# Attention on one Trainium2 core: the first scores of a step issued at the end of the step ahead

## The chip, the cores and the metric

The kernel runs on one core of a Trainium2 chip. The metric is the device time of one execution in microseconds (us); lower is better. Engines are named as in the profile: PE is TensorE (PEld its weight loads), DVE is VectorE, ACT is ScalarE, POOL is GpSimd, SP is SyncE.

## The reference

Two layers act on x of 1024 rows by 1024 columns. Cut to what matters here:

```python
for l in range(2):
    proj = rmsnorm(x, g_mix[l]) @ w_in[l]
    # A, 4 heads: softmax(q1 k1) - lam * softmax(q2 k2), all keys up to the row's chunk of 64
    # B, 4 heads: keys of a window of 128 and a sink logit
    # C, 4 heads: all keys up to the row, with a cumulated forget gate as bias
    x = x + concat([o_a, o_b, o_c]) @ w_out[l]
    h = rmsnorm(x, g_mlp[l])
    x = x + square(relu(h @ w_up[l])) @ w_down[l]
return rmsnorm(x, g_final)
```

Every softmax needs the maximum of its row of biased scores before the exponentials, and every product here is made of three fp32r products (high by high, high by low, low by high).

## The kernel before

Only the attention part of a layer is touched. It goes through 64 steps t. A step is one block of 128 query rows (i = t % 8) of one pair of score maps (t // 8): pairs 0 and 1 are group B, 2 and 3 group C, 4 to 7 group A. A row block i sees i + 1 key blocks of 128 (two at most in B), so a step has up to 1024 keys; above 512 keys its scores are made in two phases, since one map has one bank of PSUM per phase (`scores(t, 0)` and `scores(t, 1)`, line 1992).

For each step the work is: scores on PE (L2005, in C also a masked part, L2010); on DVE `biased_max` (line 1406: two L1428 instructions that add the bias, write the sum to `probs` and keep the row maximum, then L1443); on ACT two exponentials in place (L1040); on DVE in group A `combine` (L1451, L1453, L1456), which makes one map of the two; on PE transposes of the result (`turn_half`, L2058) by halves of at most four blocks; ACT copies a half as its high part (`half_high`, L1058), DVE makes the low part (`half_low`, L1479), PE multiplies by the values (`values`, L2078, L2088, L2090), and DVE sums the result (`sum_values`, L1494 in group A). In group C the result is folded on DVE first (`fold_values`, L1485) and turned on PE (`turn_values`, L2099) before it is summed.

The engines run in order, each by a list of slots that the program lays out ahead (the loop over `slots`). A slot is one half to be turned; a step has one to six slots, and the halves turned in the slots of step t are those of step t - 1. Group B and the short rows of A and C have one slot a step. `PIECES` spreads pieces of dense work over the slots: a piece is six 128x128 by 512 products (L1925) of the input projection for a later pair or of the output projection. In steps 53 to 55 and 61 of each layer (`MIX_AT`) further slots turn finished outputs for the output projection (L1053 on ACT, L1474 on DVE). After steps 51 and 58 (`SCALE_AT`) the variances of finished heads are made on DVE (L1510, L1513) and their root on ACT (L1080).

In a slot PE does: first scores if the slot is the step's first, one or two pieces, the second scores if it is theirs (`s.second`), the other pieces, `turn_values`, `turn_half` of this slot's half, `values` of the half turned one slot earlier. Pieces are split by

```python
early = max(min(2, len(s.pieces)), len(s.pieces) - 1)
```

DVE does in a slot: `biased_max(t, 0)` if first, `combine` or `invert_sums` of step t - 1 if first, the maxima of the second phase, low parts and evacuations of the projection, `half_low`, sums and folds, and in some steps the variances. ACT does, in steps with i of 4 and more, `half_high` ahead of the exponentials, in the others behind them and behind the sums' follow-up.

Semaphores that matter here: PE's scores of a phase wait until DVE has read the phase before it (`scores_read`; the two maps have one PSUM tile, ps[0]). `biased_max(t, ...)` waits until the last half of step t - 2 has been turned, since it overwrites that step's `probs`. `turn_half` in group A waits for `combined`, in B and C for the exponential; `turn_values` waits for `folded`; `values` waits for the low part.

Of the kernel before, what the change touches and what calls it, by code (L numbers as in the profile page):

```python
# [19 lines left out]
class Half:  # L20


    def __init__(self, index, step, units, slab=None, side=0):
        self.index, self.step, self.units, self.slab, self.side = index, step, units, slab, side
        self.blocks = sum(n for _, _, n in units)
        self.last = False
        self.used = None
        self.frees = 0


class Slot:


    def __init__(self, step, first, half):
        self.step, self.first, self.half = step, first, half
        self.values = None
        self.pieces, self.ends, self.ended, self.split = [], None, None, []
        self.turns_v = None
        self.summed = None
        self.unfold = None  # L40
        self.stored = None
        self.exps = []
        self.second = False


def hybrid_encoder(nc, x, w_in, a_lambda, a_subln, b_sinks, c_fbias, w_out, g_mix, g_mlp,
# [10 lines left out]
    NQ = S // P  # L57
# [55 lines left out]
    NT = PAIRS * NQ  # L113
# [86 lines left out]
    def folds(t):  # L200
        return ORDER[t // NQ][0] == "C"

    def load_of(done):
        return done if done < EXTRA else done + 1

    last = None
    for n, s in enumerate(slots):
        s.values = last.half if last and last.half and last.half.slab is None else None
        if s.values and s.values.last:
            s.summed = s.values.step  # L210
        s.unfold = last.summed if last and last.summed is not None and folds(last.summed) else None
        s.stored = []
        if last and last.unfold is not None:
            s.stored.append(last.unfold)
        if last and last.summed is not None and not folds(last.summed):
            s.stored.append(last.summed)
        if last and last.ends is not None:
            s.ended = last.ends
            n2 = load_of(last.ends + 2)
            slots[n + 2 if n2 == EXTRA + 1 else n].split.append(n2)  # L220
            if last.ends + 2 == EXTRA - 1:
                extra = slots[n + 3]
        last = s
# [46 lines left out]
    for g in range(STEPS):  # L270
# [7 lines left out]
        for name, spent in wanted:  # L278
            if kinds(g) == (P4, P4):
                t = 0 if name == "A22" else 3  # L280
            else:
                t, turn = turn % 4, turn + 1
# [15 lines left out]
    with ExitStack() as ctx:  # L298
# [980 lines left out]
        def _(dve):  # L1279
# [65 lines left out]
            for l in range(DEPTH):  # L1345
# [122 lines left out]
                def half_low(half):  # L1468
                    dve.wait_ge(pt_hi_done, NHALF * l + half.index + 1)
                    bank = bank_of(l, half)  # L1470
                    src = ps[2][:, BANK * bank:BANK * bank + half.blocks * P]
                    if half.slab is not None:
                        c = chunk_of(half.slab)
                        V.scalar_tensor_tensor(out=wide_lo[here][:, half.slab, at_slab(half)], in0=src,  # L1474
                                               scalar=mix_gain[:, NC * l + c:NC * l + c + 1],
                                               in1=wide_hi[here][:, half.slab, at_slab(half)].bitcast(F32),
                                               op0=ALU.mult, op1=ALU.subtract).then_inc(pt_split, 1)
                        return
                    V.tensor_tensor(pt_lo[:, bank, 0:half.blocks], src.rearrange("p (b q) -> p b q", q=P),  # L1479
                                    pt_hi[:, bank, 0:half.blocks].bitcast(F32), ALU.subtract).then_inc(pt_split, 1)  # L1480
# [45 lines left out]
                for s in slots:  # L1526
                    t = s.step
                    if s.first and t == 2 * NQ:
                        dve.wait_ge(cum_out, 16 * (l + 1))
                    if s.first and t < NT:  # L1530
                        biased_max(t, 0)
                    if s.first and t:
                        if ORDER[(t - 1) // NQ][0] == "A":
                            combine(t - 1)
                        else:
                            invert_sums(t - 1)
                    if s.turns_v is not None:
                        part_low(s.ended)
                    if s.second:
                        biased_max(t, 1)  # L1540
                    if s.ended is not None and s.ended < IN and s.turns_v is None:
                        part_low(s.ended)
                    if s.ends is not None:
                        if s.ends < IN:
                            evacuate(s.ends)
                        else:
                            add_out(s.ends - OUT)
                    if s.half:
                        half_low(s.half)
                    if s.unfold is not None:  # L1550
                        sum_values(s.unfold)
                    if s.summed is not None:
                        if folds(s.summed):
                            fold_values(s.summed)
                        else:
                            sum_values(s.summed)
                    if l == 0 and t == NQ and s.first:
                        lambdas()
                    if t in SCALE_AT and s.first:
                        variances(*SCALE_AT[t])  # L1560
                    if t - 1 in SCALE_AT and s.first:
                        invert_heads(*SCALE_AT[t - 1])
# [338 lines left out]
        def _(pe):  # L1901
# [40 lines left out]
            for l in range(DEPTH):  # L1942
# [71 lines left out]
                def dense(pieces):  # L2014
                    for s, c in pieces:
                        if s < IN:
                            if c == 0:
                                pe.wait_ge(w_split, LOADS * l + s + 1)
                                if SLABS[s - 1][1] == V_ and s > 4:
                                    pe.wait_ge(split_done, NSPLIT * l + s - 1)  # L2020
                                else:
                                    pe.wait_ge(evacuated, EVACS * l + s)
                            piece(s, c, 1)
                            continue
                        if c == 0:
                            pe.wait_ge(w_split, LOADS * l + s + 1)
                            if s == OUT:
                                pe.wait_ge(split_done, NSPLIT * l + NSPLIT)
                            else:
                                pe.wait_ge(evacuated, EVACS * l + s)  # L2030
                        if s == OUT:
                            pe.wait_ge(pt_split, NHALF * l + mix_ready[c])
                        j = w_slot(l, s)
                        mm = accumulate(1, w_hi[:, j, chunk_of(c)], w_lo[:, j, chunk_of(c)], wide_hi[here][:, c],
                                        wide_lo[here][:, c], c == 0, c == LATE - 1)
                        if c == LATE - 1:
                            mm.then_inc(slab_done, 1)
# [69 lines left out]
                for s in slots:  # L2107
                    t = s.step
                    early = max(min(2, len(s.pieces)), len(s.pieces) - 1)
                    if s.first and t < NT:  # L2110
                        scores(t, 0)
                    if s is slots[0]:
                        pe.wait_ge(evacuated, EVACS * l + 4)
                        turn(part, ps[3], NQ, v_turned)
                    if s.turns_v is not None:
                        pe.wait_ge(evacuated, EVACS * l + slab_of(s.turns_v, V_) + 1)
                        turn(part, ps[1], NQ, v_turned)
                    dense(s.pieces[:early])
                    if s.second:
                        scores(t, 1)  # L2120
                    dense(s.pieces[early:])
                    if s.unfold is not None:
                        turn_values(s.unfold)
                    if t == NT:
                        if s.first:
                            pe.wait_ge(scores_read, NPHASE * (l + 1))
                            pe.wait_ge(w_split, LOADS * l + EXTRA + 2)
                        for slab in (0, 1) if s.first else (2, 3):
                            out_piece(4, slab, 0, slab == 0, False)
                    if s.half:  # L2130
                        turn_half(s.half)
                    if s.values:
                        values(s.values)
# [161 lines left out]
```

## Time and profile before

| what | value |
|---|---|
| median of 3 runs | 2497.49 us (2489.79, 2498.4, 2497.49) |
| the profiled execution | 2490.63 us |
| its span, first to last instruction | 2488.5 us |
| PE busy, weight loads | 2379.5 us (96%), 1930.1 us (78%) |
| DVE busy | 1701.5 us (68%) |
| ACT busy | 1126.5 us (45%) |
| POOL busy | 260.3 us (10%) |
| mean granted clock of PE | 0.989 of full speed |
| the chain that ended last, by engine | PE 78%, DVE 9%, issue 4%, ACT 4%, DMA 2%, DVE's queue 2% |

Busy time is what an engine's instructions took, as a share of the span. The chain that ended last is followed back from the last instruction, at each step to what released it or to the instruction ahead of it on its engine. In the span, attention runs from about 69 to 556 us in layer 0 and from about 1300 to 1794 us in layer 1.

### The profile page before, as it was taken

Reading aid. Unit: us, or ns where it says so; the run is one execution under the profiler, and the core shown is the slowest. Engines: PE = TensorE matmul, PEld = TensorE weight load, DVE = VectorE, ACT = ScalarE, POOL = GpSimd, SP = SyncE. Lnnn points to the kernel's source line nnn. Section 1 sums busy time; section 2 is a strip of 40 time slices with the busy share of each in tenths; the row PEclk is TensorE's granted clock in tenths of the full one; section 3 lists DMA queues with packets and bytes.
Section 4 is the critical chain, followed back from the end, with each engine's and each line's share of the span. In section 5 each row is a group of like instructions: output and inputs, shape, how many; then the busy total and the mean of one; then the engine's idle time right before and its main releaser. Section 6 shows DMA issues by size and latency. Waiting matters only on the chain.

```text
span 2488.5 us, 32771 instructions
## 1 busy us (share of the span) xinstructions
PE 2379.5 (96%) x11857; PEld 1930.1 (78%) x11857; DVE 1701.5 (68%) x3128; ACT 1126.5 (45%) x2008; POOL 260.3 (10%) x286
## 2 busy tenths in 40 slices
PE   8999999899899999999999999998999999999998
PEld 6877777678788887888888777776787888788886
DVE  5555666666877779888636556666577777797872
ACT  5554444554544444333436545454454444433334
POOL 1111011123000000000321111121220000000002
PEclk9999999999999999999999999998999999999999
DMA  5211001211354458868331100102115544687753
GB/s 183 68 27 26 18 26 34 69 52 35 115 199 157 143 198 260 259 199 257 127 94 26 26 26 21 31 26 68 56 44 168 186 145 156 235 266 237 221 177 102
DMA packets 291400, 296.58 MB, mean 119 GB/s; under 512 B 19702, under 2 KB 236832, under 8 KB 290984
## 3 DMA queue, kind: packets, MB, share of 16 engines
q1 hardware_dynamic: 285440, 278.74, 35.3%
q10 hardware_dynamic: 5800, 15.75, 1.7%
q8 instruction: 95, 1.56, 0.3%
q14 instruction: 65, 0.53, 0.1%
HBM read 214.20 MB, written 80.25 MB: 118 GB/s over the span
## 4 chain that ended last, share of the span: by engine, by line
PE 78%; DVE 9%; issue 4%; ACT 4%; DMA 2%; DVEq 2%; SPq 1%; ACTq 0%; POOL 0%; POOLq 0%
PE ps L1925 25%; PE ps L2192 18%; PE ps L2244 8%; PE ps L2246 8%; PE ps L2245 8%; PE ps L2058 3%; PE ps L2005 3%; PE ps L2088 2%; PE ps L2078 1%; DVE probs L1428 1%; ACT pt_both L1058 1%; DVE probs L1456 1%; ACT probs L1040 1%; PE ps L2090 1%; DMA a_raw<-in_w_up_dram 1%
## 5 line engine op out<-in xcount | busy, mean ns | idle before, releaser
L2244 PE MATMUL ps<-b_hi,d_hi 128*128 128x512 f32 x896 | 351.1, 392 | 10.9 <-DVE b_lo L1721 6.5
L1925 PE MATMUL ps<-wide_hi,w_hi 128*128 128x512 f32 x1024 | 337.4, 411 | 13.5 <-DVE c_parts L1367 5.5
L2245 PE MATMUL ps<-b_lo,d_hi 128*128 128x512 f32 x896 | 350.1, 391 | 0.0
L2246 PE MATMUL ps<-b_hi,d_lo 128*128 128x512 f32 x896 | 349.7, 390 | 0.0
L1925 PE MATMUL ps<-wide_lo,w_hi 128*128 128x512 f32 x1024 | 320.1, 394 | 0.0
L1925 PE MATMUL ps<-wide_hi,w_lo 128*128 128x512 f32 x1024 | 318.5, 392 | 0.0
L1479 DVE TENSOR_TENSOR pt_both<-ps,pt_both 128x512 fp32r<-128x512 f32 (+3 forms) x216 | 126.5, 586 | 222.8 <-ACT pt_both L1058 222.1
L1162 ACT ACTIVATE d_hi<-d_raw 128x1024 fp32r<-128x1024 f32 x112 | 118.3, 1058 | 340.9 <-DVE d_raw L1705 110.4
L1058 ACT ACTIVATE pt_both<-ps 128x512 fp32r<-128x512 f32 (+3 forms) x216 | 110.4, 511 | 337.9 <-PE ps L2058 337.5
L1040 ACT ACTIVATE probs<-probs,neg_max,slope 128x256 f32<-128x256 f32 (+7 forms) x256 | 202.3, 791 | 95.2 <-DVE neg_max L1443 74.9
L883 POOL TENSOR_TENSOR w_lo<-w_raw,w_hi 128x256 fp32r<-128x256 f32 x216 | 158.2, 764 | 830.1 <-ACT w_hi L933 830.1
L1925 PEld LDWEIGHTS ps<-wide_lo,w_hi 128*128 128x128 f32 x1024 | 193.9, 189 | 43.8
L1925 PEld LDWEIGHTS ps<-wide_hi,w_lo 128*128 128x128 f32 x1024 | 193.3, 189 | 43.3
L1925 PEld LDWEIGHTS ps<-wide_hi,w_hi 128*128 128x128 f32 x1024 | 175.7, 190 | 64.7 <-issue 34.0
L2244 PEld LDWEIGHTS ps<-b_hi,d_hi 128*128 128x128 f32 x896 | 168.7, 188 | 50.4 <-DVE d_lo L1716 7.2
L2192 PE MATMUL ps<-t_hi,a_hi 128*128 128x512 f32 x472 | 188.6, 400 | 11.5 <-ACT c_rows L1140 6.6
L2246 PEld LDWEIGHTS ps<-b_hi,d_lo 128*128 128x128 f32 x896 | 169.0, 189 | 35.6
L2245 PEld LDWEIGHTS ps<-b_lo,d_hi 128*128 128x128 f32 x896 | 168.9, 189 | 34.7
L2192 PE MATMUL ps<-t_hi,a_lo 128*128 128x512 f32 x472 | 185.6, 393 | 0.0
L2192 PE MATMUL ps<-t_lo,a_hi 128*128 128x512 f32 x472 | 185.1, 392 | 0.0
L1716 DVE TENSOR_TENSOR d_lo<-d_raw,d_hi 128x1024 fp32r<-128x1024 f32 x112 | 139.8, 1249 | 41.2 <-ACT d_hi L1162 41.1
L1129 ACT ACTIVATE c_rows<-c_rows 128x512 f32<-128x512 f32 x120 | 75.7, 631 | 177.7 <-DVE c_rows L1657 176.3
(212 smaller groups left out, 4476.4 us busy)
## 6 DMA issues: line engine op xcount, KB each, us to landing
d_raw<-in_w_down_dram SPq DMA_DIRECT2D x112, 512.0 KB, 6.3
b_raw<-b_saved SPq DMA_DIRECT2D x112, 512.0 KB, 6.6
a_raw<-in_w_up_dram SPq DMA_DIRECT2D x60, 512.0 KB, 4.1
b_saved<-c_rows SPq DMA_DIRECT2D x118, 256.0 KB, 3.0
w_raw<-in_w_in_dram SPq DMA_DIRECT2D x92, 256.0 KB, 3.3
b_saved<-far SPq DMA_DIRECT2D x30, 512.0 KB, 4.3
w_raw<-in_w_out_dram SPq DMA_DIRECT2D x36, 256.0 KB, 3.0
x_saved<-xt ACTq DMA_DIRECT2D x16, 512.0 KB, 3.4
```

Of the source, the lines that this page charges most:

```text
L883: low = nc.gpsimd.tensor_tensor(w_lo[:, j, c:c + 2], w_raw[:, c:c + 2], w_hi[:, j, c:c + 2].bitcast(F32), ALU.subtract)
L1040: e = A.activation(probs[:, (2 * t + j) % 4, 0:width], probs[:, (2 * t + j) % 4, 0:width], ACT.Exp, bias=neg_max[:, at:at + 1], scale=sl, ...
L1058: A.activation(pt_hi[:, bank, 0:half.blocks], src.rearrange("p (b q) -> p b q", q=P), ACT.Copy).then_inc(pt_hi_done, 1)
L1129: A.activation(c_block[l][b], c_block[l][b], ACT.Square).then_inc(u_squared, 1)
L1162: A.activation(d_hi[u % 3][:], d_raw[t][:], ACT.Copy).then_inc(d_hi_done, 1)
L1479: V.tensor_tensor(pt_lo[:, bank, 0:half.blocks], src.rearrange("p (b q) -> p b q", q=P), pt_hi[:, bank, 0:half.blocks].bitcast(F32), ALU.s ...
L1716: V.tensor_tensor(d_lo[u % 3][:], d_raw[t][:], d_hi[u % 3][:].bitcast(F32), ALU.subtract).then_inc(d_split, 1)
L1925: mm = T.matmul(ps[p][:, bass.ts(t, BANK)], w, h[:, bass.ts(t, BANK)], start=(start and n == 0), stop=(stop and n == 2))
L2192: mm = T.matmul(out, w, h[:, c], start=(start and c == 0 and k == 0), stop=(c == NC // 2 - 1 and k == 2), skip_group_check=not start)
L2244: T.matmul(out, w0, b0, start=first, stop=False)
L2245: T.matmul(out, w0, b1, start=False, stop=False)
L2246: mm = T.matmul(out, w1, b0, start=False, stop=last)
```

## The change

For every step t with t % 8 other than 0 and t < 64 (56 steps in each layer) the first scores of the step are issued in the last slot of step t - 1: on PE behind that slot's pieces, ahead of its `turn_values`, `turn_half` and `values`. Their maxima are taken in the same slot on DVE: behind its `half_low` and ahead of its sums and folds. The first slot of step t leaves both out. Nothing else is moved; no instruction is added or left out.

```diff
+        self.early = None
+        self.scored = False
...
+        if s.first and s.step < NT and s.step % NQ:
+            last.early, s.scored = s.step, True
...
-                    if s.first and t < NT:
+                    if s.first and t < NT and not s.scored:
                         biased_max(t, 0)
...
                     if s.half:
                         half_low(s.half)
+                    if s.early is not None:
+                        biased_max(s.early, 0)
                     if s.unfold is not None:
                         sum_values(s.unfold)
...
-                    if s.first and t < NT:
+                    if s.first and t < NT and not s.scored:
                         scores(t, 0)
...
                     dense(s.pieces[early:])
+                    if s.early is not None:
+                        scores(s.early, 0)
                     if s.unfold is not None:
                         turn_values(s.unfold)
```

## Rows read from the trace of the kernel before

**Rows 1.** PE's waits: engine, line, whom it waited for, us in total, times, longest.

```profile
PE ps L2058 <- DVE probs L1456: 19.9, 24, 1.9
PE ps L2099 <- DVE fold L1485: 11.2, 12, 2.7
...
PE ps L2005 <- DVE row_max L1428: 6.2, 8, 1.5
```

**Rows 2.** DVE's waits, the line of the maxima.

```profile
DVE probs L1428 <- issue: 44.0, 61, 4.8
```

**Rows 3.** Timeline, a half of four blocks, steps 36 and 37: start, us, engine, line.

```profile
326.55 0.60 PE L2058 MATMUL ps<-ident_r,probs 128*128 128x128 f32 x4
...
327.19 0.60 ACT L1058 ACTIVATE pt_both<-ps 128x512 fp32r<-128x512 f32 x1 [4.76 <-PE ps L2058]
...
327.81 0.69 DVE L1479 TENSOR_TENSOR pt_both<-ps,pt_both 128x512 fp32r<-128x512 f32 x1 [0.56 <-ACT pt_both L1058]
...
330.57 0.89 DVE L1456 SCALAR_TENSOR_TENSOR probs<-probs,lam_ratio 128x640 f32<-128x640 f32 x1
...
332.11 0.66 PE L2058 MATMUL ps<-ident_r,probs 128*128 128x128 f32 x4
```

**Rows 4.** Timeline, a half of one block, steps 37 and 38.

```profile
334.91 0.27 PE L2058 MATMUL ps<-ident_r,probs 128*128 128x128 f32 x1
...
335.52 0.29 DVE L1479 TENSOR_TENSOR pt_both<-ps,pt_both 128x128 fp32r<-128x128 f32 x1 [1.07 <-ACT pt_both L1058]
...
335.98 0.50 PE L2005 MATMUL ps<-k_hi,q_hi 64*128 64x512 f32 x2
...
336.88 0.73 PE L1925 MATMUL ps<-wide_hi,w_hi 128*128 128x512 f32 x2
...
337.00 0.69 DVE L1428 CUSTOM_DVE_ANT_0 probs<-ps,far 128x512 f32<-128x512 f32 x1 [1.18 <-issue]
...
339.97 0.63 PE L2058 MATMUL ps<-ident_r,probs 128*128 128x128 f32 x4 [0.74 <-DVE probs L1456]
```

**Rows 5.** Timeline of PE, four waits in last slots (steps 20, 28, 29, 61).

```profile
181.01 0.44 PE L2099 MATMUL ps<-ident_r,fold 128*128 128x128 f32 x2 [0.28 <-DVE fold L1485]
...
259.03 0.44 PE L2099 MATMUL ps<-ident_r,fold 128*128 128x128 f32 x2 [1.43 <-DVE fold L1485]
...
270.13 0.74 PE L2078 MATMUL ps<-pt_both,c_parts 128*128 128x256 f32 x4 [1.18 <-DVE pt_both L1479]
...
530.25 0.39 PE L2088 MATMUL ps<-v_parts,pt_both 128*128 128x256 f32 x1 [1.04 <-DVE pt_both L1479]
```

**Rows 6.** Timeline, folds and the turns that wait for them, steps 18 to 27.

```profile
167.85 0.68 DVE L1485 TENSOR_REDUCE fold<-ps 128x256 f32<-128x512 f32 x1
...
170.74 0.38 PE L2099 MATMUL ps<-ident_r,fold 128*128 128x128 f32 x2
...
243.07 0.68 DVE L1485 TENSOR_REDUCE fold<-ps 128x256 f32<-128x512 f32 x1
...
244.24 0.38 PE L2099 MATMUL ps<-ident_r,fold 128*128 128x128 f32 x2
...
249.48 0.44 PE L2099 MATMUL ps<-ident_r,fold 128*128 128x128 f32 x2 [2.69 <-DVE fold L1485]
```

**Rows 7.** Timeline of ACT and DVE, steps 59 and 60.

```profile
511.04 1.28 ACT L1040 ACT_TABLE_LOAD   x1
...
514.36 0.47 ACT L1058 ACTIVATE pt_both<-ps 128x384 fp32r<-128x384 f32 x1
...
515.78 0.69 DVE L1428 CUSTOM_DVE_ANT_0 probs<-ps,far 128x512 f32<-128x512 f32 x1
...
518.98 0.35 DVE L1428 CUSTOM_DVE_ANT_0 probs<-ps,far,row_max 128x128 f32<-128x128 f32 x1 [0.16 <-issue]
```

**Rows 8.** Windows: stretch, us, busy (x) of PE, PEld, DVE, ACT, POOL, PEclk, DMA, GB/s.

```profile
451.50:455.00 3.50, 3.49 (x17) 3.50 (x18) 2.03 (x7) 2.26 (x7) 3.50 (x6) 0.51 0.00 0
478.60:482.00 3.40, 2.01 (x14) 1.32 (x14) 3.15 (x10) 0.70 (x2) 0.22 (x1) 1.00 0.59 166
```

## The prediction

> **What bounds the kernel now.** I read the page first: PE is busy 2379.5 us of the 2488.5 us span, so all idle time of PE is 109 us, and nothing that leaves PE's own work alone can win more. The table of PE's waits then says what part of it this change can reach [rows 1]: 19.9 us in 24 waits of the transposes for `combine`, 11.2 us in 12 waits for folds, 6.2 us in 8 waits of second scores for the maxima of the first phase. That is 37.3 us over both layers, 1.5% of the time. DVE's table shows 44.0 us of idle time in front of the maxima, 61 times [rows 2]: DVE was free and PE had not yet made the scores. That is what moving the scores forward speaks to. Whether it helps has to be read from the timeline, slot by slot, because DVE works in order and its list hardly changes: the maxima stood directly behind `half_low` and the last slot's sums already, and are now only put ahead of those sums. On PE the scores change places with `turn_half` and `values` of one slot. So the question is which of two chains feeds the maxima last.
>
> **The change part by part.** The instructions stay the same, no DMA is moved, and SP's and POOL's queues are not passed; all that is to be priced is waiting.
>
> The basic exchange. First scores of 512 keys take 0.97 us (335.98 to 336.95; six matmuls) and a piece 1.4 us (336.88 to 338.3) [rows 4]. Before, the maxima began when `turn_half`, `values` and scores had all gone through PE; now they begin when scores, `turn_half`, `half_high` and `half_low` are through. For a last half of four blocks [rows 3]: the turn ends at 327.15, ACT takes 0.60, DVE 0.69, so `half_low` ends at 328.50. With scores first, all three come 0.97 later, so the maxima start at about 329.45 where they started at 328.76, and the exponentials of step 36, which ACT has behind `half_high`, are late too. `combine` ended at 331.46 with its turn at 332.11, a margin of 0.65; the sum in front of it does not get shorter, so it ends about 1.1 later, near 332.55, and PE waits about 0.5 to 0.6: a wait where none was. For a last half of one block [rows 4]: `half_low` ended at 335.81, the maxima waited 1.18 us until 337.00. Scores first, the short half is ready by about 336.5, half a us earlier, and the 0.74 us wait at 339.97 and the one of the second scores ahead of it shrink by about as much. Following the four-slot pattern through steps 37, 38 and 39 (and 45 to 47 alike) I get +0.6, -0.5, +0.1 us: **+0.2 us** for each of two pairs.
>
> Waits that the moved scores fill. In a last slot PE now has 0.97 us more to do ahead of `turn_values` and `values`. Four waits a layer lie there [rows 5]: 0.28 us at 181.01 is filled whole, of the 1.43 at 259.03 about 0.95, of the 1.18 at 270.13 about 0.85 (the turn comes late by that much, but ACT reaches it no sooner). Of the 1.04 at 530.25 some 0.9 is filled, but `combine` of step 61 does not move and is waited for next, so 0.5 is kept. **-2.6 us.**
>
> Folds behind the maxima. Where a step of group C has one slot, the fold stands behind the early maxima: 1.3 us, L1443 with its drain 0.5, and 0.97 for the turn that is late. The fold at 167.85 ends at 168.53, its turn starts at 170.74, a margin of 2.2; the fold now ends near 171.65. PE waits 0.95 and then the chain of step 20's second scores carries it on: **+0.9 us.** The fold at 243.07 has a margin of 0.5 only [rows 6]; it ends near 246.85, a wait of 2.4 us at 244.24. But 2.69 us were lost at the next turn, at 249.48, because `half_high` stood behind two exponentials; these start only 0.5 later, so most of that wait has gone by. I get the turn at 250.35 with step 28's first scores done, where it was 249.48 with them to come: **-0.95 us** for the two.
>
> Root, table load and the second maxima, steps 59 and 60. This is the largest term. In step 58's slot the variances now stand behind the maxima of step 59 (1.3 us, L1443 0.3) and behind a `half_low` that is 0.4 late: 2 us. ACT's root waits for them, its load of the exponential's table (1.28 us, from 511.04) follows, and then two exponentials and `half_high` at 514.36 [rows 7], all 2 us later. So `half_low` and the maxima of step 60 go from 515.78 to about 517.4. And step 60 has its second scores and the early scores of step 61 in one slot with two pieces, both of which stand ahead of the second scores: step 61's scores wait for the second maxima of step 60, which stand behind `combine` of step 59 on DVE (518.98 before [rows 7], about 521.1 now). PE waits until about 521.8 with `turn_half`, `values`, dense pieces and through them `half_low` queued behind. The turn starts near 522.65; it was 518.96, and the scores, which then came behind it, are 0.97: 2.7 us lost here. One slot on, `half_low`, maxima and `combine` in a row are late by 1 us more. **+3.7 us.** In steps 36, 44 and 52 one piece lies between the two scores; its 1.4 us covers the second maxima, with 0.4 us to spare in the first.
>
> Steps 51 to 54. In step 51 the variances are behind the maxima too, second maxima of step 52 end 0.3 late for PE, and `half_high` and with it the exponentials of step 52 come 1.3 later; the 1.9 us wait, the longest on `combine` [rows 1], grows by as much: **+1.3 us.** In step 54 a mix half of four blocks is the last: **+0.4 us.** In step 55 ACT is last as before: 0. Groups B and the steps with three pieces have more than 2 us of cover for the late half: 0; without it each of these would cost up to 0.5.
>
> The clock. Behind the 1.9 us wait [rows 1] the granted clock is 0.51 from 451.5 to 455.0, the lower level of 1.2 GHz; behind the longest wait on the maxima, 1.5 us [rows 1] up to 478.6, it stays at 1.00 [rows 8]. The half-speed stretch costs about 1.7 us of 3.5. The wait of some 2.4 us before step 61's scores has no row of its own; it is nearer to the first of the two, but it need not hit, so I take half: **+0.9 us**; bounds 0 and 1.7, and with the longer waits of steps 27 and 53 up to 3.4. The Trainium skill ("TensorE: Matmul & The Clock Gate", the part on HAM oscillation) speaks of longer gaps than any named here as what costs the clock. By it this term is 0 and the sum 1.8 us lower. The trace does not agree, by its row behind the 1.9 us wait.
>
> **Sum** for a layer: 0.4 - 2.6 + 0.9 - 0.95 + 3.7 + 1.3 + 0.4 + 0.9 = +4.05 us; layer 1 shows the same waits (12 of the 24, 6 of the 12), so **+8.1 us**, 0.33%. Against the profiled execution this is 2490.6 + 8.1 = 2498.7. That execution was 6.9 us under the median of the runs shown, and the four times lie in two groups, 2490 and 2498; their mean is 2494.1. I put the sum on that mean: **2502 us**.
>
> **The rivals.** (a) The exchange is a gain where I read a loss: DVE's 44 us of idle time goes, and with it most of the 37.3 us of [rows 1]. If only the terms that gain count and half of the `combine` and maxima waits (13 us) go too: 2.6 and 0.95 twice is 7.1, in all -20 us, 2474. For it: 61 idles. Against it: the half of one block is the only kind in which `half_low` was long done. (b) Slower by a new wait at one place: early scores behind the second maxima, in single-slot steps 36, 44, 52 and 60. It decides once `combine` ends later than one piece behind the second scores. Step 60 has no piece; if the three others also lose 1 to 1.5 us each, and the clock drops behind each, this adds 3 to 5 us a layer: 2510 to 2513 on the mean. (c) The change does nothing, since DVE's order is almost what it was, and step 60's table load is hidden after all: 2494, within 2 us.
>
> **How the numbers follow.** My forecast, a small loss of 4 to 12 us, has 0.5; (c) with what lies around it, down to -10 us, 0.24; (a) 0.1; (b) 0.16. A difference of 0.5% (12.5 us) is about what a measurement of this kernel can tell from no change. Faster than that takes (a): 0.1. Slower takes (b) in full: 0.16. Within: 0.74. The range goes from 2486 (a gain of 4 on the lower group) to 2513 (b's end).
>
> **What would show it.** Right, if PE's waits for folds include one of over 2 us near step 27, if PE's L2005 waits for `far_max` of L1428 in step 60 (there is no such wait now), if the variances of step 58 (L1510, L1513) start only behind the L1443 of step 59, and the table load with them, and if DVE's idle time ahead of L1428 falls far below 44 us while the waits for L1456 do not fall by more than a third. Wrong, if the waits for L1456 fall below 8 us, or if step 60's turn is not late by 2 us or more against step 57's.

## The result and the profile after

The changed kernel takes 2508.26 us in the median of 6 runs (2505.92 to 2511.84); the kernel before took 2494.73 us in 6 runs on the same occasion. The ratio is 1.0065, 95% interval 1.0051 to 1.0078: slower by 12.7 to 19.5 us (the two medians alone lie 13.5 us apart). The forecast, 2502 in a range of 2486 to 2513, had the sign and held the time; its sum of +8.1 us was about half of what came.

The page of the changed kernel, its span and busy times:

```profile
span 2504.0 us, 32771 instructions
## 1 busy us (share of the span) xinstructions
PE 2386.3 (95%) x11857; PEld 1925.1 (77%) x11857; DVE 1700.6 (68%) x3128; ACT 1127.6 (45%) x2008; POOL 261.1 (10%) x286
```

The instructions are the same in number, and the span is 15.5 us longer. It parts in two. PE idle is 2504.0 - 2386.3 = 117.7 us where it was 2488.5 - 2379.5 = 109.0: **8.7 us more waiting**. PE busy is up by **6.8 us** with the same matmuls: these took longer. The forecast had 6.3 us of waits and 1.8 us of clock.

The stretch of attention in both layers, before and then changed, between the same instructions (columns as in [rows 8]):

```profile
69.30:556.10 486.80, 455.89 (x2679) 363.05 (x2680) 305.73 (x919) 250.86 (x589) 79.91 (x109) 0.99 0.13 39
1300.00:1794.00 494.00, 464.77 (x2711) 371.04 (x2710) 303.22 (x904) 248.12 (x582) 77.08 (x105) 0.99 0.13 36
```

```profile
69.30:561.80 492.50, 459.08 (x2679) 360.33 (x2680) 305.27 (x919) 251.35 (x589) 80.30 (x109) 0.98 0.13 38
1306.00:1809.00 503.00, 469.17 (x2712) 369.24 (x2711) 303.08 (x904) 248.69 (x582) 77.49 (x105) 0.98 0.12 36
```

The layers lost 5.7 and 9.0 us there. Waits are 2.5 and 4.6 of it, 7.1 in all; the other 1.6 of the 8.7 us lie outside what was changed. PE's busy time makes 3.2 and 4.4, 7.6 in all, at a lower granted clock.

PE's waits of the changed kernel, to be read against [rows 1] (lines are shifted by 4 to 8: L1460 is `combine`, L1432 the maxima, L1489 the fold, L1044 an exponential, L2064 the transposes, L2011 scores, L2105 the turn of a fold, L2094 values):

```profile
PE ps L2064 <- DVE probs L1460: 22.4, 30, 2.5
PE ps L2011 <- DVE row_max L1432: 14.0, 19, 1.5
...
PE ps L2094 <- DVE pt_both L1483: 4.6, 8, 1.0
PE ps L2105 <- ACT probs L1044: 4.6, 2, 2.3
...
PE ps L2105 <- DVE fold L1489: 4.1, 10, 0.8
...
PE ps L2011 <- DVE far_max L1432: 3.4, 2, 1.7
```

The waits for folds fell from 11.2 us to 4.1, with 4.6 beside them that are put down to an exponential: 2.5 us won. The waits of values fell. But the waits for `combine` did not fall (22.4 where 19.9 were), those for the first maxima more than doubled (14.0 for 6.2), and the wait for the second maxima, `far_max`, is new. DVE's own table shows what the change did do:

```profile
DVE probs L1432 <- issue: 18.5, 26, 3.3
```

DVE's idle time ahead of the maxima is down from 44.0 us to 18.5 [rows 2]. None of the 25.5 us came out as time. They were DVE's and not PE's.

Timeline of the changed kernel in steps 36 and 37, the steps of [rows 3]:

```profile
323.12 0.50 PE L2011 MATMUL ps<-k_hi,q_hi 64*128 64x512 f32 x2
...
324.02 0.66 PE L2064 MATMUL ps<-ident_r,probs 128*128 128x128 f32 x4
...
325.35 0.69 DVE L1483 TENSOR_TENSOR pt_both<-ps,pt_both 128x512 fp32r<-128x512 f32 x1 [1.61 <-ACT pt_both L1062]
325.96 0.69 DVE L1432 CUSTOM_DVE_ANT_0 probs<-ps,far 128x512 f32<-128x512 f32 x1
...
328.10 0.89 DVE L1460 SCALAR_TENSOR_TENSOR probs<-probs,lam_ratio 128x640 f32<-128x640 f32 x1
...
329.13 0.63 PE L2064 MATMUL ps<-ident_r,probs 128*128 128x128 f32 x4 [0.46 <-DVE probs L1460]
```

Read it from turn to `combine`: 324.02 to 328.10 is 4.08 us; before, it was 326.55 to 330.57, 4.02 us [rows 3]. The chain turn, `half_high`, `half_low`, maxima, sum, `combine` is as long as ever. It starts 0.9 us later against PE's own list, since the scores now stand in front of the turn, and a wait of 0.46 us stands where a margin of 0.65 was.

### The profile page after: what moved, and what is told of

Its sections match the earlier page's. It is cut to its first block, busy times and chain, and to the rows that moved or that the text cites. A ratio compares the mean times of both kernels' runs of the same rounds, so it can differ in the third digit from the quotient of the medians.

```text
span 2504.0 us, 32771 instructions
## 1 busy us (share of the span) xinstructions
PE 2386.3 (95%) x11857; PEld 1925.1 (77%) x11857; DVE 1700.6 (68%) x3128; ACT 1127.6 (45%) x2008; POOL 261.1 (10%) x286
## 4 chain that ended last, share of the span: by engine, by line
PE 77%; DVE 10%; issue 4%; ACT 4%; DMA 2%; DVEq 2%; SPq 1%; ACTq 0%; POOL 0%; POOLq 0%
PE ps L1931 23%; PE ps L2200 18%; PE ps L2252 8%; PE ps L2253 8%; PE ps L2254 8%; PE ps L2064 4%; PE ps L2011 3%; PE ps L2094 2%; DVE probs L1432 1%; ACT pt_both L1062 1%; DVE probs L1460 1%; DMA d_raw<-in_w_down_dram 1%; PE ps L2084 1%; PE ps L2096 1%; ACT probs L1044 1%
## 5 line engine op out<-in xcount | busy, mean ns | idle before, releaser
L2252 PE MATMUL ps<-b_hi,d_hi 128*128 128x512 f32 x896 | 351.2, 392 | 10.4 <-DVE b_lo L1727 6.3
L1044 ACT ACTIVATE probs<-probs,neg_max,slope 128x256 f32<-128x256 f32 (+7 forms) x256 | 202.2, 791 | 73.0 <-DVE neg_max L1447 57.3
```

The source lines that it names most:

```text
L1044: e = A.activation(probs[:, (2 * t + j) % 4, 0:width], probs[:, (2 * t + j) % 4, 0:width], ACT.Exp, bias=neg_max[:, at:at + 1], scale=sl, ...
L2252: T.matmul(out, w0, b0, start=first, stop=False)
```

## The experiments

In the diffs, the two lines that issue the early scores on PE, and the two that take their maxima on DVE, are those of the change. All ratios are to the kernel before, measured beside the run. "Idle" is PE's, span less busy of the profiled execution; before it is 109.0 us.

**One group of steps at a time.** The first of two, group C alone:

```diff
-        if s.first and s.step < NT and s.step % NQ:
+        if s.first and s.step < NT and s.step % NQ and ORDER[s.step // NQ][0] == "C":
```

> Early scores only for the steps of group C (i 1 to 7 in pairs 2 and 3, 14 steps a layer); A and B as before. My theory (the loss is made in group A by scores ahead of the turn, and by the clock): PE's waits fall by 1 to 2 us a layer against the kernel before, with fold waits at 8 to 9 us where they were 11.2 and the waits of values (L2078, L2088) down by 2 us a layer; the time is 2 to 5 us below before, 0.998 to 0.9995, if the half-speed stretches do not grow. Rival (maxima ahead of the folds are what costs): fold waits above 11 us and the time 3 us or more above before. Rival (the early scores cost wherever they stand, as PE changes its pattern): half of the 15.5 us, 7 us above before.

Measured: 0.998 (0.9965 to 0.9995), median 2488.99 us; idle 106.9. Group C alone is a gain, as forecast. Its fold waits (4.1 us, and 4.6 put down to the exponential) are those of the changed kernel; of the waits of values, group C's own 2.4 us (L2084, before L2078) are gone, 1.2 a layer and not 2: those on L2094, 7.7 us, are group A's. The second, group A alone (the same line with "A"):

> Early scores only for the steps of group A (28 a layer); B and C as before. My theory: the whole loss is here and more than whole, since C gained: 16 to 20 us above before, ratio 1.0065 to 1.008, with the wait for far_max (L1428) of 1.7 us a layer, a combine wait of 2.5 us near step 53 and at least 10 us more time at half speed than before. Rival (the fold order costs): no more than 8 us above before.

Measured: 1.0047 (1.0031 to 1.0064), 2505.95 us; idle 119.4, 10.4 above before. The loss is in group A, with the `far_max` wait (3.4 us in 2) and the longest `combine` wait (2.5 us) as said, but 11.7 us is less than the 16 to 20 I named. With C's -5 and A's +11.7 us the parts add to +6.7, under the whole's +16; the intervals are some 4 us wide each side and group B, which was not run alone, adds something (below). The waits do add up: idle -2.1 and +10.4, the whole +8.7. What is missing shows in the granted clock, as the mean over all executions of a kernel: 0.989 before and in group C alone, 0.987 in group A alone, 0.985 in the changed kernel.

**Where the scores stand on PE.**

```diff
-                    if s.early is not None:
-                        scores(s.early, 0)
                     if s.unfold is not None:
                         turn_values(s.unfold)
...
                     if s.half:
                         turn_half(s.half)
+                    if s.early is not None:
+                        scores(s.early, 0)
                     if s.values:
                         values(s.values)
```

> The early scores are issued behind turn_half of the last slot, ahead of its values, instead of ahead of both; DVE's list as in the changed kernel. My theory: what makes the maxima late is that the turn of the last half, and with it half_high, half_low and in the later steps the exponentials, stand 0.97 us behind the scores. With the turn first, combine waits fall from 22.4 us to 10 to 14 us and row_max waits from 14.0 to under 7; steps 59 to 61 keep about 2.5 us a layer of their loss (table load behind the variances). The time is 10 to 16 us under the changed kernel: 2492 to 2498, ratio to before 0.999 to 1.002. Rival (the loss is DVE's order, or the fixed pattern of PE): within 4 us of the changed kernel, 1.005 and more.

Measured: 0.9967 (0.9949 to 0.9984), 2485.52 us, faster than before and some 23 us under the changed kernel. Idle 98.2. Its waits:

```profile
PE ps L2064 <- DVE probs L1460: 19.9, 24, 2.0
...
PE ps L2094 <- DVE pt_both L1483: 6.2, 8, 1.1
PE ps L2105 <- DVE fold L1489: 5.9, 12, 1.5
```

The waits for the first maxima are 4.6 us in 4, none for `far_max`. The theory held, and more strongly than I had put it: the ratio lies below the range I gave. One number missed the other way: waits for `combine` are 19.9 and not 10 to 14. Timeline of the same steps as above:

```profile
321.78 0.60 PE L2064 MATMUL ps<-ident_r,probs 128*128 128x128 f32 x4
...
323.04 0.69 DVE L1483 TENSOR_TENSOR pt_both<-ps,pt_both 128x512 fp32r<-128x512 f32 x1 [0.56 <-ACT pt_both L1062]
...
325.80 0.88 DVE L1460 SCALAR_TENSOR_TENSOR probs<-probs,lam_ratio 128x640 f32<-128x640 f32 x1
...
327.42 0.66 PE L2064 MATMUL ps<-ident_r,probs 128*128 128x128 f32 x4
```

Turn to `combine` is 4.02 us again, and the next turn comes with a margin, as before the change. The same kernel once more, since it beats both:

> The third run's kernel once more, in more rounds, since it may beat both kernels. My theory: ratio to before 0.9955 to 0.998, 5 to 11 us under before. Rival (its first result was the clock's luck in the executions drawn): 0.999 to 1.001.

Measured: 0.9964 (0.9951 to 0.9978), 2483.29 us; idle 98.9. The first result was not luck.

**DVE's order.** PE as in the changed kernel, the early maxima behind sums, folds and variances:

```diff
                     if s.half:
                         half_low(s.half)
-                    if s.early is not None:
-                        biased_max(s.early, 0)
...
                     if t - 1 in SCALE_AT and s.first:
                         invert_heads(*SCALE_AT[t - 1])
+                    if s.early is not None:
+                        biased_max(s.early, 0)
```

> PE as in the changed kernel; on DVE the early maxima stand behind the slot's sums, folds and variances instead of ahead of them, so DVE's list is that of the kernel before. My theory: this takes back the table load's lateness in steps 59 to 61 (2 to 2.5 us a layer) and the new fold waits, but gives the maxima 0.4 us later in group A: 4 to 8 us under the changed kernel, ratio to before 1.003 to 1.005; the wait for far_max stays, at 0.7 to 1.2 us. Rival (DVE's order is the whole loss): back to before, 0.999 to 1.001. Rival (it is not DVE's order at all): 1.0065.

Measured: 1.0053 (1.0036 to 1.0071), 2509.13 us; idle 119.6. No gain can be told from the changed kernel. The waits for folds give nothing back, they are 10.7 us now where 4.1 and 4.6 were; the later maxima take more too (15.9 us for `row_max`, 14.0 before this edit). The `far_max` wait stayed at 1.55 us each, more than I gave it. So DVE's order is not the loss. The same order with the turn ahead of the scores:

> Scores behind turn_half; on DVE the early maxima behind the slot's sums, folds and variances, so that DVE's list is that of the kernel before and the change is PE's order alone. My theory: the maxima start as early as half_low and the scores allow, less 0.4 us for a sum: most of the gain is PE's order. Ratio to before 0.996 to 0.9985, combine waits 1 to 4 us above the third run's 19.9. Rival (the maxima ahead of the sums make the gain): 1.000 or more.

Measured: 0.9993 (0.998 to 1.0006), 2491.93 us; idle 105.0. Here my theory was too simple. With DVE's list as before, moving the scores behind the turn gives nothing that can be told from no change; the gain of 8 to 9 us needs the maxima ahead of the sums too. Its fold waits are 11.3 us where the third run has 5.9 and 2.0. The reason shows in DVE's waits: the sums wait for `values`, which PE now reaches only behind the early scores. DVE waits 18.1 us in 27 for them, where it waits 3.7 us in 2 in the third run, and the maxima stand behind. In steps 36 and 37:

```profile
325.25 0.60 PE L2064 MATMUL ps<-ident_r,probs 128*128 128x128 f32 x4
...
327.62 0.42 DVE L1498 TENSOR_REDUCE o_out<-ps 128x128 f32<-128x256 f32 x1 [0.42 <-PE ps L2096]
...
329.78 1.24 DVE L1460 SCALAR_TENSOR_TENSOR probs<-probs,lam_ratio 128x640 f32<-128x640 f32 x1
...
331.17 0.63 PE L2064 MATMUL ps<-ident_r,probs 128*128 128x128 f32 x4 [0.20 <-DVE probs L1460]
```

Turn to `combine` is 4.53 us here.

**Steps 59 to 61.** First without them:

```diff
-        if s.first and s.step < NT and s.step % NQ:
+        if s.first and s.step < NT and s.step % NQ and s.step not in (59, 61):
```

> The changed kernel, but the first scores of steps 59 and 61 stay in their own step. My theory (3 to 3.7 us a layer are lost by the variances standing behind step 59's early maxima and by step 61's early scores waiting for the second maxima of step 60): the wait for far_max (3.4 us in 2) is gone, PE's idle time falls by 4 to 7 us, and the time is 5 to 8 us under the changed kernel: ratio to before 1.002 to 1.004. Rival (all of it is clock, set off anywhere): PE's idle time falls as said but the time stays within 2 us of the changed kernel, since the half-speed stretches come elsewhere.

Measured: 1.0034 (1.0021 to 1.0047), 2501.49 us, 6.8 us under the changed kernel; idle 114.0, 3.7 less, just under the 4 to 7 I gave; the `far_max` wait is gone. In time the place costs about what I said. Then its first half alone, the variances ahead of the early maxima:

```diff
+                    if t in SCALE_AT and s.first:
+                        variances(*SCALE_AT[t])
                     if s.early is not None:
                         biased_max(s.early, 0)
```

> The changed kernel with the variances of steps 51 and 58 ahead of the early maxima on DVE, so that ACT's root and table load are released as early as half_low allows; all else as in the changed kernel. My theory: in steps 59 to 61 the exponentials and half_high come 1.6 us sooner, which saves 1.5 to 2 us a layer there (the wait for far_max shrinks to 0.8 to 1.2 us), and 0 to 0.4 us a layer at step 52: 3 to 5 us under the changed kernel, ratio 1.0035 to 1.0055. Rival (the second maxima behind combine are the whole loss in steps 60 and 61, table load hidden): within 1 us of the changed kernel.

Measured: 1.0048 (1.0032 to 1.0064), 2507.16 us; idle 116.8, 0.9 less. Timeline of PE in the changed kernel, its waits in steps 59 to 61 of layer 0:

```profile
521.96 0.33 PE L2011 MATMUL ps<-k_hi,q_hi 64*128 64x128 f32 x2 [0.78 <-DVE row_max L1432]
524.19 0.50 PE L2011 MATMUL ps<-k_hi,q_hi 64*128 64x512 f32 x2 [1.68 <-DVE far_max L1432]
530.20 0.63 PE L2064 MATMUL ps<-ident_r,probs 128*128 128x128 f32 x4 [0.26 <-DVE probs L1460]
```

and in this run:

```profile
522.41 0.50 PE L2011 MATMUL ps<-k_hi,q_hi 64*128 64x512 f32 x2 [1.09 <-DVE far_max L1432]
...
526.60 0.39 PE L2011 MATMUL ps<-k_hi,q_hi 64*128 64x256 f32 x2 [0.55 <-DVE row_max L1432]
528.41 0.91 PE L2064 MATMUL ps<-ident_r,probs 128*128 128x128 f32 x4 [1.19 <-DVE probs L1460]
```

Step 61's scores come 1.8 us sooner (522.41 for 524.19), 1.4 of it from the waits ahead of them, as forecast. The waits of 0.55 and 1.19 us behind them look new, but they are not this edit's. In the changed kernel the granted clock is 0.50 from 525.7 to 529.1, and the slower matmuls fill that time. In its layer 1, at full clock, the same waits stand, and the edit leaves them as they are. Layer 1, changed and this run:

```profile
1755.95 0.50 PE L2011 MATMUL ps<-k_hi,q_hi 64*128 64x512 f32 x2 [1.68 <-DVE far_max L1432]
1760.14 0.39 PE L2011 MATMUL ps<-k_hi,q_hi 64*128 64x256 f32 x2 [0.54 <-DVE row_max L1432]
1761.95 0.63 PE L2064 MATMUL ps<-ident_r,probs 128*128 128x128 f32 x4 [1.19 <-DVE probs L1460]
```

```profile
1750.97 0.51 PE L2011 MATMUL ps<-k_hi,q_hi 64*128 64x512 f32 x2 [1.06 <-DVE far_max L1432]
1755.17 0.39 PE L2011 MATMUL ps<-k_hi,q_hi 64*128 64x256 f32 x2 [0.56 <-DVE row_max L1432]
1756.98 0.68 PE L2064 MATMUL ps<-ident_r,probs 128*128 128x128 f32 x4 [1.19 <-DVE probs L1460]
```

From the turn two steps ahead (517.43 and 1749.18 in the changed kernel) to the last turn shown is 12.77 us in both layers of the changed kernel, and 11.3 in both of this run: 1.5 us a layer won at the place. Over the kernel that is 3 us, and the intervals can't tell it from nothing. With the turn ahead of the scores the same edit gave:

> The scores behind turn_half as in the third run, and the variances ahead of the early maxima. My theory: the third run still lost about 1.1 us a layer in steps 59 to 61; this takes 0.8 to 1.1 us of it back: 1 to 3 us under the third run, ratio to before 0.995 to 0.997. Rival (nothing of the variances is left once the turn is early): the same as the third run, 0.9967.

Measured: 0.9967 (0.9955 to 0.998), 2485.53 us; idle 101.4. The ratio is the third run's, as the rival has it, but a gain of 1 to 3 us is less than the interval, so the time decides nothing. The traces show the small gain at the place: between the same two turns 10.6 us pass here in both layers (511.95 to 522.52 in layer 0), 11.4 in the third run (507.79 to 519.19). And with step 61's scores left in their step as well:

> Scores behind turn_half, variances ahead of the early maxima, and step 61's first scores left in their own step. My theory: with the turn ahead of them step 61's early scores hold up only values, and the wait for the second maxima of step 60 is one that the turn behind them had anyway (combine ends 0.1 ahead of those maxima): so leaving them out wins at most 0.5 us a layer. Ratio to before 0.9955 to 0.9975, the same as the eighth run within 1 us. Rival (that wait costs there as it did in the changed kernel): 2 us or more under the eighth run.

Measured: 0.9957 (0.9943 to 0.997), 2482.89 us; idle 97.7. The best of all, though it can't be told from the third run's kernel (0.4 us under it on the same occasion). By the ratios it is 2.5 us under the eighth run, more than I gave and what the rival said, with intervals some 3 us wide each side: this stays open.

**Steps 53 to 55 alone**, for the clock:

```diff
+        if s.first and s.step < NT and s.step % NQ and s.step in (53, 54, 55):
```

> Early scores for steps 53, 54 and 55 alone (6 of the 112). My theory: PE's waits there grow by 1.7 us a layer (1.3 in step 53, 0.4 in step 54, 0 in step 55), and the rest of the 5.6 us that the changed kernel's layer 0 loses between steps 52 and 55 is time at half speed, which follows from the longer waits: PE idle 3 to 4 us above before, granted clock in the stretch of steps 53 to 55 under that of before in at least one layer, time 3 to 9 us above before, ratio 1.001 to 1.0035. Rival (the clock falls where it will, whatever the waits): +3 to +4 us with PE busy within 1 us of before. Rival (the waits alone are larger than read): PE idle 8 us or more above before, PE busy unchanged.

Measured: 1.0027 (1.001 to 1.0044), 2501.85 us; idle 114.0, 5.0 above before, of which 3.4 are the waits for `combine` (21.0) and `row_max` (8.5). Six moved steps of 112 cost 2.5 to 11 us. The windows around those steps in both layers, before, changed, this run, and the third run, one after another:

```profile
440.00:500.00 60.00, 48.99 (x294) 38.50 (x291) 40.59 (x109) 31.10 (x63) 10.77 (x16) 0.97 0.22 71
1660.00:1730.00 70.00, 59.87 (x329) 47.13 (x328) 43.03 (x117) 33.06 (x70) 13.60 (x20) 0.90 0.19 61
```

```profile
440.00:500.00 60.00, 48.02 (x264) 37.56 (x262) 36.09 (x95) 28.71 (x58) 10.76 (x16) 0.89 0.22 71
1660.00:1730.00 70.00, 58.05 (x301) 45.12 (x300) 41.38 (x110) 32.70 (x70) 11.58 (x17) 0.85 0.21 68
```

```profile
440.00:500.00 60.00, 49.31 (x259) 38.58 (x257) 34.98 (x88) 29.75 (x61) 10.72 (x16) 0.83 0.19 62
1660.00:1730.00 70.00, 57.98 (x312) 45.03 (x309) 43.91 (x118) 33.95 (x72) 13.57 (x20) 0.90 0.21 68
```

```profile
440.00:500.00 60.00, 48.85 (x294) 38.27 (x292) 37.88 (x101) 31.29 (x66) 12.72 (x19) 0.97 0.22 71
1660.00:1730.00 70.00, 58.51 (x340) 45.52 (x340) 43.34 (x122) 33.79 (x72) 13.71 (x20) 0.98 0.21 68
```

The column behind the five engines is the granted clock. In the first window it is 0.97 before and 0.83 here, in the second 0.90 in both. It isn't fixed by the code alone: in the run of group C alone, whose group A is that of before, these two read 0.91 and 0.98. So one layer bears the theory out, the other doesn't, and no single execution settles it. The executions taken together do: the mean granted clock is 0.987 over the 10 of this run and 0.989 over the 24 of the kernel before beside them. The rival with PE's busy time unchanged doesn't hold either, it is up by 8.3 us in the profiled execution.

## Why the prediction was right, and what was off

**The mechanism held.** The forecast's reading, that the maxima were never free of `half_low` and that the turn pays for what the scores gain, is what the runs show: 4.0 to 4.1 us from turn to `combine` in steps 36 and 37, with the turn behind the scores a loss, with the turn in front a gain. It was too simple in one point: with the turn in front and the maxima behind the sums it is 4.5 us, and the gain is gone.

**The waits, term by term.** Forecast +6.3 us, measured +8.7, of which 7.1 in the attention parts.
- *Step 37 and its like*, +0.6: the 0.46 us wait at 329.13 and the lost margin. That steps 38 and 39 give it back was wrong in size: the 0.74 us wait of [rows 4] is still 0.49, and step 39's waits are what they were (0.40 and 0.78). A pair loses 0.7 to 0.8 us and not 0.2.
- *Waits that the scores fill*, -2.6: right in kind. The wait of 0.28 at 181.01 is gone, the 1.43 at 259.03 is 0.55, and those at 270.13 and 530.25 [rows 5] are gone. Beside them stand waits for the first maxima that weren't there, 0.66 us at 179.00 and 0.59 at 252.87. So the waits of group C fell by 1 us a layer (the run of C alone, -2.1 for both), where the forecast's terms for C add to -2.1 a layer.
- *Folds behind the maxima*, +0.9 and -0.95: the new wait for the fold of step 16 is 0.80 us (forecast 0.95), and the long one near step 27 is there:

```profile
246.25 0.44 PE L2105 MATMUL ps<-ident_r,fold 128*128 128x128 f32 x2 [2.29 <-ACT probs L1044]
```

  2.29 us for a forecast 2.4, in place of 2.69 [rows 6]. The view puts it down to an exponential, but the fold itself ends 0.06 us ahead of that turn (245.51, 0.68 us long). The forecast's sum for the first of these folds was off: its parts give 171.3 and not 171.65.
- *Steps 59 to 61*, +3.7: from the timeline, the turn of step 60 in step 61's first slot went from 524.05 to 530.20, and the one two steps ahead from 513.69 to 517.43 with 0.97 us of scores now in front of it: 6.15 - 2.77 = 3.4 us. Layer 1 has the same 3.4 (1749.18 to 1761.95 where 1736.22 to 1746.58 was), there all of it as waits; in layer 0 some 1.5 us of it is matmuls at the lower clock. The rows of the chain, against [rows 7]:

```profile
516.42 1.28 ACT L1044 ACT_TABLE_LOAD   x1
...
519.62 0.47 ACT L1062 ACTIVATE pt_both<-ps 128x384 fp32r<-128x384 f32 x1
```

  Load to `half_high` is 3.20 us, before 3.32; with the kernel's own lateness at this point (2.8 us) taken off, both are some 2.5 us later than they were, for the 2 worked out.
- *Step 53*, +1.3: the longest `combine` wait is 2.48 us, before 1.90, with a new 0.56 us for the maxima ahead of it. Together +1.14.
- *Not priced*: step 14 of group B. I gave B nothing. Its exponentials come late, ACT's copy of the next V part stands behind them, and the wait for it goes from 0.94 to 1.01 us with a new one of 0.37 in front; the dense piece at 144.23 stands at 144.92, 0.7 us a layer.

**The term that failed is the clock.** "The clock ... so I take half: +0.9 us" a layer, for one place. PE's busy time rose by 6.8 us. In layer 0 it rose in steps 53 to 57, where I had waits of 0.4 and 0 for steps 54 and 55: the turn at 465.86 came 0.4 us early in the changed kernel, at 465.44; the one at 480.33 came 1.2 late, at 481.49; the one at 494.23 was 3.4 late, at 497.58. In the window of 440 to 500 us the granted clock is 0.89 where it was 0.97, and in layer 1 0.85 where it was 0.90. I had looked at a single wait behind which the clock fell, and priced only a new wait of that length; this stretch has nine waits of 0.5 to 1.5 us within some 25 us, before as after, and the row that I used as the case in which nothing happens (1.00 behind 1.5 us, [rows 8]) did not hold: in the changed kernel the wait of 1.47 us at 479.74 has the clock at its lower level of 1.2 GHz just behind it, the next transposes taking 1.08 us for 0.63.

```profile
479.74 0.51 PE L2011 MATMUL ps<-k_hi,q_hi 64*128 64x512 f32 x2 [1.47 <-DVE row_max L1432]
481.49 1.08 PE L2064 MATMUL ps<-ident_r,probs 128*128 128x128 f32 x4 [0.77 <-DVE probs L1460]
```

Two places more speak against the way I priced it. The first is in the trace of before: the 1.9 us wait that I took the price from has a twin in layer 1, at 1670.55, and behind that one the clock stays at 1.00; it falls there behind waits of 0.8 and 1.5 us, as the second and third line show.

```profile
1670.50:1674.00 3.50, 3.36 (x26) 3.11 (x27) 1.97 (x7) 2.70 (x8) 3.50 (x6) 1.00 0.02 5
1683.80:1690.60 6.80, 6.24 (x24) 5.32 (x24) 2.87 (x8) 3.78 (x7) 0.00 (x0) 0.50 0.00 0
1700.90:1707.70 6.80, 6.24 (x24) 5.15 (x23) 2.46 (x7) 2.50 (x4) 0.00 (x0) 0.50 0.94 302
```

The second is the place that I did price, step 60's. The clock fell there in layer 0 and not in layer 1, the half chance that I gave it, but it cost nothing: 12.77 us pass between the two turns in both layers, since PE at full clock waits for the chain of ACT and DVE instead.

The Trainium skill ("TensorE: Matmul & The Clock Gate", the part on HAM oscillation) has longer gaps than these as the cause; by that part's rule the term would have been 0, farther off still. The same page of the Trainium skill (on what is actually happening) says of the slow matmuls at a kernel's start that their number varies between runs of one kernel. The runs here show such a variation in later stretches too, below.

**What the kernels show together.** Change of idle time against change of time (ratio by 2494 us): -10.8 and -8 us (third run), -10.1 and -9 (again), -7.6 and -8 (with the variances first), -11.3 and -11 (with 61 left out), -2.1 and -5 (C alone), -4.0 and -2 (DVE as before), +5.0 and +7 (53 to 55), +5.0 and +8 (without 59 and 61), +7.8 and +12 (variances first, scores ahead), +8.7 and +16 (changed), +10.4 and +12 (A alone), +10.6 and +13 (DVE as before, scores ahead). Waiting sets the sign; within the losing side it doesn't set the order, and each us of it came with up to 0.9 us more. The split is no finer than a few us: PE is busy 2382.8 us in the profile of the kernel run again and 2379.5 before, at clocks of 0.991 and 0.989.

**The rivals.** (a) fell: DVE's idle time went and PE's waits did not. (b), early scores behind second maxima, decides in step 60 alone, as the forecast had it; in steps 36, 44 and 52 one piece covers it but for the 0.56 us before step 53's. (c) fell.

That the clock's part belongs to the change and not to the execution that was profiled, the executions show: the granted clock is 0.984 to 0.987 in the six of the changed kernel, mean 0.985, and 0.985 to 0.992 in 70 of the kernel before, mean 0.989. An estimate from these two means is 17 us more at half speed, which is at most 9 us of time; 13.5 us between the medians less 8.7 us of idle time leave about 5. The kernels with turn and maxima first have a mean of 0.990. What stays open is which waits bring the clock down.

## What to carry to other kernels

When work of an in-order engine is moved ahead, look at what it is moved in front of: here 0.97 us of scores in front of a short transpose delayed a 4 us chain by all of it, and the same scores behind the transpose made a gain of 9 us out of a loss of 16. Idle time in front of an instruction is worth nothing unless the bound engine waits behind it; and an engine's freed time shows up only if both ends, PE's order and DVE's, are set for it. Where PE already waits in short pieces close together, price a further wait at more than its length, and don't take the clock's reading from one profiled execution.

## What the runs showed of the hardware

The granted clock fell behind waits of 1.5 us and less in one execution and not in another with the same instructions there: in the window of 440 to 500 us it read 0.97 before and 0.91 in the run that leaves this part as it was. In layer 1 it was the other way round, 0.90 and 0.98. Executions of one kernel differ along with it: of 24 of the kernel before on one occasion the shortest, 2487.3 us, has a clock of 0.992, and the longest, 2501.05 us, one of 0.986. That is more than most single steps of this study are worth.

A stretch at half speed need not cost time on an engine that waits for others: 3.4 us of it in steps 59 to 61 of the changed kernel's layer 0 left the time between two turns at the 12.77 us of layer 1.
